# Recording the mixer of a hybrid RG-LRU / Conformer layer in three overlapping stages

## The reference, cut to what matters

```
h = modulate(x, ffn1_g, sh1, sc1)
x = x + 0.5 * gt1 * swiglu(h, ffn1_wg, ffn1_wu, ffn1_wd)          # FFN1

h = modulate(x, mix_g, sh2, sc2)
z_lx, z_lg, z_cv, z_cg = split(h @ w_in)                          # 4 x 512 channels
y = causal_dwconv(z_lx, width 4)                                  # group A
r, i = sigmoid(block_diag(y, wa)), sigmoid(block_diag(y, wx))
a = exp(-8 * r * softplus(-lam));  b = sqrt(1 - a*a) * i * y
h_t = a_t * h_(t-1) + b_t                                         # scan over time
lru = h_t * gelu(z_lg)
u = z_cv * sigmoid(z_cg)                                          # group B
v = silu(layer_norm(causal_dwconv(u, width 31)))
x = x + gt2 * concat(rms_norm(lru), rms_norm(v)) @ w_out

h = modulate(x, ffn2_g, sh3, sc3)
x = x + 0.5 * gt3 * swiglu(h, ffn2_wg, ffn2_wu, ffn2_wd)          # FFN2
y = rms_norm(x, final_g)
```

## Time and profile before

| | before |
|---|---|
| median of 3 runs | 5017.64 us |
| the runs | 4989.7, 5017.64, 5401.35 us |
| the profiled execution | 4984.06 us (span of its slowest core 4982.5) |
| PE busy | 4694.1 us (94%) |
| DVE, ACT, POOL busy | 2494.2, 2268.6, 337.7 us |
| ACT function table loads | 525, 673.6 us |
| mean granted PE clock, 8 cores | 0.979 to 0.982 |

### The profile page before, as it was taken

How to read it: one execution, slowest core, us unless ns; L and a number is a source line. 1 busy time by engine, 2 the same in 40 slices (tenths; PEclk the granted TensorE clock), 3 DMA queues, 4 the chain that set the end, 5 groups by cost and what they waited for, 6 DMA issues and landing times.

```text
span 4982.5 us, 87163 instructions; the slowest of 8 cores (4973.4 to 4982.5 us)
## 1 busy us (share of the span) xinstructions
PE 4694.1 (94%) x30312; PEld 2590.7 (52%) x30312; DVE 2494.2 (50%) x4994; ACT 2268.6 (46%) x3463; POOL 337.7 (7%) x339
## 2 busy tenths in 40 slices
PE   6989999999999998689998999999999999999998
PEld 3756444444444444465554565555555555555553
DVE  3354533334444442555564665556556556555652
ACT  2232222222222221656664655655665565666651
POOL 0100000000000000101010100101010010100000
PEclk9999999999999999899999999999999999999999
DMA  9733432322222124444554554554454455545544
GB/s 175 127 72 84 88 69 59 70 60 56 57 69 60 57 49 117 142 129 112 162 152 97 168 152 128 155 158 142 131 162 147 130 157 151 142 131 159 160 124 142
DMA packets 431853, 585.60 MB, mean 118 GB/s; under 512 B 59328, under 2 KB 250176, under 8 KB 427712
## 3 DMA queue, kind: packets, MB, share of 16 engines
q1 hardware_dynamic: 409136, 515.79, 36.4%
q0 software_dynamic: 22288, 64.24, 8.3%
HBM read 546.44 MB, written 118.12 MB: 133 GB/s over the span
## 4 chain that ended last, share of the span: by engine, by line
PE 77%; ACT 6%; DMA 5%; DVE 5%; issue 4%; SPq 2%; POOL 0%; ACTq 0%; DVEq 0%; POOLq 0%
PE ps L731 75%; PE ps L1184 2%; ACT L515 2%; DVE X L1301 2%; DMA cu<-U 1%; DMA stk<-cu 1%; SPq L1177 1%; DVE TI L1126 1%; DMA Wgu<-wgu 1%; DMA slab<-wad 1%; ACT sg L1285 1%; DVE MT L1141 0%; ACT RS L707 0%; DVE V L1205 0%; ACT TR L1106 0%
## 5 line engine op out<-in xcount | busy, mean ns | idle before, releaser
L731 PE MATMUL ps<-hT,rgu 128*128 128x512 bf16 (+2 forms) x5984 | 1320.1, 375 | 73.1 <-DVE aT L1286 41.4
L731 PE MATMUL ps<-hT,Wgu 128*128 128x512 bf16 (+1 forms) x5632 | 1179.9, 371 | 25.2 <-DVE aT L839 15.4
L731 PEld LDWEIGHTS ps<-hT,rgu 128*128 128x128 bf16 x5984 | 580.8, 99 | 713.5 <-issue 139.3
L731 PEld LDWEIGHTS ps<-hT,Wgu 128*128 128x128 bf16 x5632 | 550.6, 98 | 633.4 <-issue 37.4
L515 ACT ACT_TABLE_LOAD x525 | 673.6, 1283 | 339.1 <-PE ps L731 185.9
L731 PE MATMUL ps<-aT,rdn 128*128 128x512 bf16 (+2 forms) x2992 | 647.2, 370 | 3.2 <-DMA rdn<-wddB 3.2
L731 PE MATMUL ps<-aT,Wd 128*128 128x512 bf16 (+2 forms) x2992 | 604.5, 363 | 0.0
L839 DVE TENSOR_TENSOR aT<-ps,sgA 128x512 bf16<-128x512 f32 (+2 forms) x374 | 243.2, 651 | 624.6 <-PE ps L731 509.7
L838 ACT ACTIVATE sgA<-ps 128x512 bf16<-128x512 f32 (+2 forms) x396 | 219.3, 555 | 712.1 <-PE ps L731 637.9
L731 PE MATMUL ps<-hTm,Win 128*128 128x256 bf16 (+1 forms) x4224 | 495.8, 272 | 1.4 <-ACT TR L1094 1.2
L1286 DVE TENSOR_TENSOR aT<-ps,sg 128x512 bf16<-128x512 f32 (+2 forms) x374 | 246.6, 662 | 457.8 <-PE ps L731 274.1
(11 more groups left out here) (152 smaller groups left out, 3606.8 us busy)
## 6 DMA issues: line engine op xcount, KB each, us to landing
rgu<-wguB SPq DMA_DIRECT2D x748, 256.0 KB, 3.5
rdn<-wddB SPq DMA_DIRECT2D x272, 352.0 KB, 3.2
stk<-cu SPq DMA_DIRECT2D x512, 71.0 KB, 3.4
X<-x SPq DMA_DIRECT2D x32, 1024.0 KB, 8.7
yd<-X SPq DMA_DIRECT2D x30, 1024.0 KB, 7.6
x<-XA SPq DMA_DIRECT2D x26, 1024.0 KB, 4.0
XA<-xd SPq DMA_DIRECT2D x48, 512.0 KB, 5.0
hTm<-hm SPq DMA_DIRECT2D x32, 512.0 KB, 4.8
```

The lines of the kernel that those rows point to most:

```text
L731: x = e.matmul(o, lhsT=l, rhs=r, start=start and i == 0, stop=stop and i == len(pairs) - 1)
```

## The change

`mixer` now returns five lists: A (load `hTm`, the Conformer input: 64 `Win` matmuls, `U`, its DMA), La (halo, 32 `Win`, width-4 convolution, the gates `Wab`), Lb (Exp/Ln, the Gelu branch, the scan, `MT[0:4]`), Cb (the width-31 convolution to `MT[4:8]`), E (the output projection). They are recorded in steps: a front step [A(0), La(0)], and then for each tile i first [Lb(i), Cb(i), A(i+1)], then [E(i), La(i+1)]. Within a step the list that is least far along and whose banks fit goes next. `hTm` becomes double, `LX` single (its halo is copied within the buffer), and `hb` moves from `U` to `MT[4]` and `MT[5]`. A mixer operation that finds no bank is now skipped instead of forcing the order. `target` and the knots are unchanged.

```diff
-    hTm = LB("hTm", [128, 8, MN], BF16)
-    LX = [LB("LX%d" % i, [128, 4, 272], F32) for i in range(2)]
+    hTm = [LB("hTm%d" % i, [128, 8, MN], BF16) for i in range(2)]
+    lx = LB("LX", [128, 4, 272], F32)
...
-    hb = [S.sb("hb%d" % i, [128, MN], BF16, UOFF + 512 * i) for i in range(2)]
+    hb = [MT[:, 4 + i] for i in range(2)]
...
-                S.add('pool', lambda e, w=w: e.tensor_copy(out=lx[:, :, w:w + 3], in_=lxp[:, :, pl:pl + 3]))
+                S.add('pool', lambda e, w=w: e.tensor_copy(out=lx[:, :, w:w + 3], in_=lx[:, :, pl:pl + 3]))
...
-        C = S.coll = []
+        S.coll = A
         for h in range(2):
             pa, pv = bankm(), bankm()
...
+        Cb = S.coll = []
         for c in range(4):
             if len(segs) > 1 or c % 2 == 0:
                 p = bankm()
...
-        return P, L, C, E
+        return A, La, Lb, Cb, E
...
+    class Step:
+        def __init__(self, lists):
+            self.lists = [x for x in lists if x]
+            self.at = [0] * len(self.lists)
+            self.n = sum(map(len, self.lists))
+
+        def step(self):
+            c = [(self.at[k] / len(x), k) for k, x in enumerate(self.lists)
+                 if self.at[k] < len(x) and S.fits_banks(x[self.at[k]])]
+            if not c:
+                return False
+            k = min(c)[1]
+            S.put(self.lists[k][self.at[k]])
+            self.at[k] += 1
+            return True
...
+    mp = [mixer(i) for i in range(len(MIX))] + [((), (), (), (), ())]
     mx = []
-    for t in range(NF):
-        for i in mixes[t]:
-            p = mixer(i)
-            mx.append([mixed(p, t), sum(map(len, p)), t, home[i][1], MIX[i][1]])
+    for i in range(len(MIX)):
+        A1, La1 = mp[i + 1][0], mp[i + 1][1]
+        Lb, Cb, E = mp[i][2:]
+        mx.append(([Step([Lb, Cb, A1]), Step([E, La1])], home[i][0], home[i][1], MIX[i][1]))
+    front = [Step([mp[0][0], mp[0][1]])]
```

More of the change, by code:

```diff
@@ L1030, in mixer @@
         segs = segs_of(c0, nt)
-        lx = LX[i % 2]
-        lxp = LX[(i - 1) % 2]
+        hm = hTm[i % 2]
         lo = []
@@ L1053, in zmm @@
         def zmm(p, m, col):
-            mmg(lambda: p[:, col:col + nt], [(Win[:, m, k, :], hTm[:, k, 0:nt]) for k in range(8)])
+            mmg(lambda: p[:, col:col + nt], [(Win[:, m, k, :], hm[:, k, 0:nt]) for k in range(8)])
         def fold(q, out):
@@ L1065, in foldsq @@
             S.add('dve', lambda e: e.tensor_tensor(out=out[:, 0:nt], in0=fa[:, 0, 0:nt], in1=fa[:, 1, 0:nt], op=ALU.add))
-        L = S.coll = []
+        La = S.coll = []
+        for (s, o, n, b), w in zip(segs, lo):
+            if s >= 4:
+                S.add('pool', lambda e, w=w, q=s - 4: e.tensor_copy(out=lx[:, :, w:w + 3], in_=LCH[:, :, 3 * q:3 * q + 3]))
+            elif b == 0:
+                S.add('pool', lambda e, w=w: e.memset(lx[:, :, w:w + 3], 0.0))
+            else:
+                S.add('pool', lambda e, w=w: e.tensor_copy(out=lx[:, :, w:w + 3], in_=lx[:, :, pl:pl + 3]))
         for h in range(2):
@@ L1235, in mixer, with left @@
         S.coll = None
-        return P, L, C, E
+        return A, La, Lb, Cb, E
     fdone = [0]
-    def mixed(p, t):
-        P, L, C, E = p
-        for x in P:
-            yield x
-        il = ic = 0
-        while il < len(L) or ic < len(C):
-            l = ic == len(C) or (il < len(L) and il * len(C) <= ic * len(L))
-            if not S.fits_banks(L[il] if l else C[ic]):
-                l = not l
-            if l:
-                il += 1
-                yield L[il - 1]
-            else:
-                ic += 1
-                yield C[ic - 1]
-        assert fdone[0] >= t - 1, (t, fdone)
-        for x in E:
-            yield x
+    class Step:
[12 more added lines that the diff above has]
+            return True
+        def left(self):
+            return self.n - sum(self.at)
     def hp2(t, off, n):
@@ L1323, in mstep @@
         g = mx[mdone[0]]
-        S.put(next(g[0]))
-        mdone[1] += 1
-        if mdone[1] == g[1]:
+        q = front[0] if front else g[0][0] if g[0][0].left() else g[0][1]
+        if q is g[0][1] and fdone[0] < g[1] - 1:
+            return False
+        if not q.step():
+            return False
+        if front and not front[0].left():
+            front.pop()
+        if not g[0][1].left():
             mdone[0] += 1
-            mdone[1] = 0
-            pend.append(hp2(*g[2:]))
+            pend.append(hp2(*g[1:]))
+        return True
     def mpos():
-        return mdone[0] + (mdone[1] / mx[mdone[0]][1] if mdone[0] < len(mx) else 0)
+        if mdone[0] == len(mx):
+            return mdone[0]
+        a, b = mx[mdone[0]][0]
+        return mdone[0] + 1 - (a.left() + b.left()) / (a.n + b.n)
     KNOT = 0.15
@@ L1353, in follow @@
             while mdone[0] < len(mx) and mpos() < target(x):
-                mstep()
+                if not mstep():
+                    break
             while not S.fits_banks(o):
-                mstep()
+                assert mstep()
             S.put(o)
-    n0 = sum(g[1] for g in mx[:len(mixes[0])])
+    n0 = sum(q.n for g in mx[:len(mixes[0])] for q in g[0]) + front[0].n
     it = 0
```

16 lines of the change are left out of this document (5 added, 11 removed).

## The result

| | before | after |
|---|---|---|
| median | 5017.64 us (5 runs, 4988.72 to 5401.35) | 4857.58 us (5 runs, 4848.29 to 4963.98) |
| after / before | | 0.9719, interval 0.9694 to 0.9744 |
| span of the profiled execution | 4982.5 us | 4856.0 us |
| PE busy | 4694.1 us | 4632.5 us (4660.0 us in the second profile, below) |
| ACT function table loads | 525 | 469 |

The change makes the kernel 2.8% faster. The forecast was 4925 us. In some executions the cores of one die run at a lower granted clock (the run of 5401 us is one); ratios leave these out, and where a profiled execution has such a die, the cores of the other are read. The spans of the profiled executions are 126.5 us apart (4982.5 to 4856.0), where 71 were forecast.

What follows compares the result with a forecast made beforehand. The prediction took PE to be the bound (busy 4694.1 of 4982.5 us). Its terms 11 + 16 + 7 + 4 + 12 + 15 + 6 = 71 us gave 4913, forecast as a median of 4925 us, range 4845 to 4995.

Steps and rivals of the forecast that it cites:

- tile 0's hole, tiles 1 and 2 (idle 2000 to 2200): First mixer tiles: the next tile's A and La matmuls fill PE's idle time, gaining 11 and 16 us.
- 2200 to 2600: PE's 17.7 us idle time in this window: 4 us gained, bounds 0 and 17.7, FFN2's own waits staying.
- sample tile: Around 2650 us: convolution chain and its input made a stage earlier, gaining 12 of 26.0 us idle.
- steady, the mixer's own waits: Long steady stretch: `stk` nearly vanishes, `MT` and `hb` halve, gaining 15 of 21.3 us.
- steady, FFN2's waits `aT` and `sg`: Long steady stretch: fewer ACT table loads (469 for 525) take 11% off 54.5 us of waits, 6 us.
- the clock, first windows: 2000 to 2200 us: less idle time raises PE's granted clock, gaining 7 of at most 18 us.
- rival 1: Holes close almost wholly: mixer's waits vanish, FFN2's halve, 153 us gained, 4831 us; chance 0.15, whole or in part.
- rival 2: Steady stretch: projection joints wait for banks, giving back 59 us, 4972 us, or no gain there; chance 0.25.
- the "14.7 us" of "DMAs and their issue on SP": Sample tile: PE's waits at the narrow convolutions (7.3, 4.5, 2.9 us), put down to DMAs and their issue.
- the 13 that a higher price of a load is said to give: FFN2's steady waits: at about 2.7 us per table load instead of 1.283, the term would be 13, not 6.
- Its variant: Steady stretch: the scheduler, looking 900 operations ahead, already had the overlap; only first tiles gain, 4957 us.
- Rival 3: SP queue: `cu` DMAs waiting for `U` hold back FFN2's weights, PE starves 284 us, 5197 us; chance 0.05.

Runs made afterwards that it cites:

- e12: The changed kernel itself, unaltered, profiled a second time: ratio to the kernel before 0.9723, profiled span 4846.8 us.
- e5: The kernel before with the mixer's scans on DVE replaced by one product each: ratio to before 0.9921, profiled span 4944.8 us.
- e6: The kernel before with Silu in place of Gelu, so that branch needs no table load of its own: ratio to before 0.9948.
- e7: The changed kernel with two more Gelu table loads wherever one stands: profiled span 4892.9 us against the changed kernel's 4846.8; no ratio.
- e8: The changed kernel with its mixer recorded another 0.3 tile ahead of FFN2, 391 table loads: ratio to before 0.9853, against 0.9723.
- e4: The changed kernel with the gates overlap alone: La(i+1) beside E(i), A(i+1) recorded alone between: ratio to before 0.9746.
- e1: The kernel before with only the change's buffers (two hTm, one LX, hb in MT), recorded as before: ratio to before 0.9977.
- e9: The kernel before with both products for the scans and Silu for Gelu: ratio to before 0.99, profiled span 4931.6 us.

## Why the prediction was right or wrong

PE's order and its idle time of the first 2000 us are the same in both (90.3 and 89.6 us). So the account is of the second half, before against e12, which is 135.7 us shorter in span. PE's idle time fell from 198.0 to 97.1 us, and its busy time from 4694.1 to 4660.0.

| term of the sum | forecast | measured |
|---|---|---|
| tile 0's hole, tiles 1 and 2 (idle 2000 to 2200) | 11 + 16 | 57.2 to 39.2: 18 |
| 2200 to 2600 | 4 | 17.7 to 10.8: 7 |
| sample tile | 12 | 26.0 to 14.9: 11 |
| steady, the mixer's own waits | 15 | 21.3 to about 8: 13 |
| steady, FFN2's waits `aT` and `sg` | 6 | 54.5 to 0.9: 54 |
| new waits (`X`, `rgu`) in the steady stretch | 0 | -3 |
| the clock, first windows | 7 | 6 |
| the rest of the fall of PE's busy time, mostly the clock | 0 | 28 |
| sum | 71 | 134 |

**The step that failed** is "only the share of PE's waits goes: 56 of 525 is 11%, 11% of 54.5 us is 6". It took the table loads as a rate, and the waits as proportional to it. "The change doesn't touch FFN2's 4 banks" was true, and beside the point: what empties those banks stands in queues on ACT and DVE, and the change rearranges these queues. PE waits only where the gap between two `sg` or two `aT` is longer than the banks last, so what counts is how the mixer's work is bunched within a tile, and how many of its matmuls PE has to run in the meantime, not how much work there is. e5 and e6 show the two waits apart; e7 shows that a bunch of loads costs FFN2 nothing under PE's new order; e8 shows that fewer loads don't help. The term measured 54 us in place of 6. The rows for it were at hand: ten waits of 2.7 us, one per FFN2 tile, each at the same place, is the mark of a collision, not of a rate. The prediction read the earlier trace rows as totals and did not look at one of them in the timeline.

That the time still lies in the range is in good part luck. The sum has 71 of 134 us, and the range held because it took in most of rival 1's band, which had a chance of 0.15; "faster", which came, had 0.26. The 12 us that were added because a median should lie above the profiled execution didn't come: the median run of after is the profiled one.

**The clock.** For the first windows 7 us were forecast and 6 came: (1 - 0.75) x 20.1 + (1 - 0.95) x 140.7 = 12 us are left of 18. But "granted clock over 0.80 in the first 40 us" was wrong: 0.75 (0.76 in the other profile), because the hole was split and not filled. The prediction also puts the 9.51 us of 64 `Wout` matmuls down to 1.2 GHz; twice 7.15 would be 14.3, so the low level held for a part of them only. What was left out is the clock of the rest. In the steady stretch it went from 0.99 to 1.00, in the trace's third digit from 0.991 to 0.999: what the low level takes from 1940 us, (1 - clock) times the length, fell from 17 to 2 us. So once idle time vanishes, the same matmuls also run faster, and this gave back more than the first windows. Over the whole span the same reckoning gives (1 - 0.981) x 4982.5 = 95 us and (1 - 0.988) x 4846.8 = 58. The clock isn't all of the 28 us: behind each wait the last matmul's end counts as busy for some 0.16 us, and PE has 142 waits before and 88 after, an estimate of 9 us.
The Trainium skill ("TensorE: Matmul & The Clock Gate", section on the HAM clock gate) says that idle time throttles and sustained work releases. The steady stretch agrees: 1.00 at 99.4% busy, 0.99 at 96.2%. That it is worth counting where idle time is only 4% the prediction did not draw from it.

**Point by point.** Idle time from 2000 to 2200 us "down from 57 to about 30": 39, so a third of the forecast's fall is missing; the bound that warned of it ("if DVE and ACT stretch the chain by as much") was partly real. In exchange A and La of the next tile run 11.4 us of PE work ahead all through, and the last FFN2 tile but one, which has less of the mixer beside it, is 15 us shorter (159.2 to 144.1). "No wait there over 8 us": the longest is 5.4. `stk` under 3 us in the steady stretch: none. `sg` and `aT` "still 40 to 60 us": 1.2, wrong. 469 loads: yes. At most 15 us idle at the sample tile: 14.9 (17.3 in the profile with missing records). "Wrong if the idle time of the steady stretch falls below 30 us": it fell to 12. The sign of rival 2, new waits for `X`, is there as well, at 3.5 us. Two readings were off besides. Of the "14.7 us" of "DMAs and their issue on SP" at the sample tile only 4.5 are a DMA's: 2.9 are DVE's `BA`, and the 7.3 for "issue" are time in which PE waited for nothing that the profile shows. And the 13 that a higher price of a load is said to give doesn't follow, since the term is a share of the loads' number (56 of 525), in which their price doesn't enter.

**The rivals.** Rival 1 named what came, but not why: its argument was "slack" of ACT and DVE, its price for FFN2's waits was half of them, and it took the holes of the first tiles as closed, which they are not. Its sum, 153, is near the 134 only because too much there (57, where 18 came) met too little for FFN2's waits (27, where 54 came) and for the clock (12, where up to 34 came). Rival 2 is out: the joints of the projection are there (`Wout` in 117 rows of PE's order), but they cost 3.5 us in after, not 59; in e4, with other phases, they cost 15.8. Its variant, that the scheduler had the overlap of the steady stretch already, falls with the steady tile itself (176.1 to 169.7 us), and e1 shows that it doesn't find it with the new buffers either. Rival 3 is out: `rgu` 0.4 us, and SP waits less for `U` than in the earlier trace rows (perhaps because `U` is now made a stage before it is needed; no run tests this). SP's waits, 2760 to 4880 us:

```profile
SPq L513 <- DVE U L1151: 75.0, 40, 4.9
```

**What stays open.** The change parts the mixer's stages on ACT, DVE and POOL, and it mixes the mixer's matmuls among FFN2's on PE. No run does one without the other, so how much each brings isn't shown; e4 and e7 suggest that the second is enough against `sg`. That POOL's hold is the larger part of `aT`'s delay (2.0 of the 3.0 us that before needs more than e5) comes from timelines and from e5 beside e9; a version with the subtraction on DVE wasn't run. Why both overlaps together are only 0.5 us a tile better than the gates overlap alone isn't shown either, but PE's floor of 167.1 us leaves little room: 169.7 is 1.6% above it.

## What to carry to other kernels

When a nearly saturated engine waits in one long stretch, look at the single waits in the timeline before pricing them by a rate: equal waits at equal spacing are the mark of a collision of two chains in an in-order queue, and a new order can remove them whole, nearly without removing work. See also what the waiting engine runs just before: a late bank costs nothing where it has other matmuls to run in the meantime. To part stages of two loops that share ACT, DVE and POOL, record them beside phases of the other loop that use other engines (here gates beside the projection, the next input beside the recurrence); here the buffers alone brought nothing that could be measured (0.9977), and a shift of the whole mostly exchanged one wait for another (0.992). Count the clock too: idle time that is spread in small pieces costs its own length and more.
